# Forget gates' logits as four column tiles of 32 columns, in plain 32-bit, with a pattern that adds the partial sums

## The chip, the cores and the metric

One core of one Trainium2 chip runs the whole program. The metric is the device time of one execution in microseconds; smaller is better. TensorE multiplies matrices into eight banks of PSUM, VectorE (DVE) and ScalarE (ACT) work between PSUM and SBUF, GpSimd (POOL) computes and issues transfers, SyncE (SP) issues the transfers of weights.

## The reference

Two transformer blocks for 512 tokens of width 1024. The first modulates a normalised `x`, projects it and runs two attentions; the second has a convolution branch, a differential attention and a cross attention with a memory of 256 tokens. The change touches only the forget gates of the first block's first attention:

```python
h = rms_norm(x, g_pre[l]) * (1.0 + scale[:, None, :]) + shift[:, None, :]
proj = h @ w_in[l]
qa, ka, va, fa, za, qb, kb, vb, zb = jnp.split(proj, split_points, axis=-1)   # fa: 8 columns, one a head
...
cum = jnp.cumsum(jax.nn.log_sigmoid(f_logit.astype(jnp.float32)), axis=1)      # f_logit = fa + b_fgate
...
s = s + cb[..., None] - cum[:, :, None, :]
```

So the logits are `h` (512 x 1024) times eight columns of weights; their cumulated log-sigmoid is a bias on all scores of that attention.

## The kernel before

Almost all matrix products run in three matmuls of a rounded 32-bit type. Each operand is split into a high part (`hh`, `wh`) and a low part (`hl`, `wl`), and `three` adds lo x hi, hi x lo and hi x hi. The weights come in chunks of 1024 x 128 (0.52 MB), named by kind and number and listed in `CHUNKS` in the order in which they are multiplied. `("fa", 0)` holds the eight gate columns four times, at columns 0, 32, 64 and 96, with zeros between, so that the logits stand on four groups of partitions.

A chunk passes through three hands:

- SP loads it into one of four slots of `raw`, in the order of the list `RAW`, in which pieces of `w_ada` stand between chunks. SP's queue is one and strictly in order. A slot's next load waits until VectorE has split what was in it (`w_lo`), or, for a piece of `w_ada`, has added it up (`ada_used`). The names that share a slot here: `("va", 0)` follows the first chunk of the stage, `("va", 1)` the second; the order is chunk, chunk, `ada` 16, `ada` 17, `("va", 0)`, `("va", 1)`, `ada` 18, `ada` 19, `("va", 2)`, `("va", 3)`.
- ScalarE writes `wh` (its function `ahead`, L1126), then VectorE `wl` (its own `ahead`, L1800; the pieces of `w_ada` at L1781). Both go through their lists in order and stop only where the slot of `wh` and `wl` is not yet used up, so `ahead(name)` splits the chunk that stands four behind `name`.
- TensorE multiplies it: `chunk` takes eight times `three`, 24 matmuls of 512 columns. The four chunks `va` are multiplied in `wide`, where each step of 24 matmuls uses one chunk for all four tiles of tokens.

At the start of the first attention TensorE runs `fa`, `qa`, four steps of `va`, `ka`, then two plain 32-bit matmuls for the output gate (L652), then pieces of the chunks in `FILL` between the units of attention. The first scores wait for `cum_done`. In the meantime VectorE adds the bias to the logits (L1883), ScalarE takes absolute value, exponential and logarithm (L1282 to L1287), and VectorE the cumulated sum (L1889). ScalarE reads `qa` into `qf` and splits it (`raw_q`, L1294, and `split_q`, L1305).

GpSimd's queue in this stage: after `h_lo` it loads `sel` (its memory is that of `x` and `xT`, the scaled input in plain 32-bit) and twice `wmask`, then it stores `kvm`, 2 MB, to DRAM (L1046), then it computes angles.

`Banks` counts for each PSUM bank how often it was filled and emptied: `open` lets TensorE wait until the bank is empty, `wait_full` and `wait_empty` let others wait for it. `next_bank` hands out banks 0 and 1 in turn. Each engine executes its instructions in the order in which they stand.

Of the kernel before, what the change touches and what calls it, by code (L numbers as in the profile page):

```python
# [33 lines left out]
P = 128  # L34
# [18 lines left out]
K_COLS = K_DIST + S  # L53
# [14 lines left out]
CHUNKS += [("fa", 0), ("qa", 0)] + [("va", j) for j in range(4)] + [("ka", 0)]  # L68
# [71 lines left out]
for _h in range(4):  # L140
# [6 lines left out]
    "ones_in": "ones loaded", "sq_hi": "differential outputs' squares: hi", "sq_lo": "lo",  # L147
# [70 lines left out]
def constants():  # L218
    k = np.zeros((P, K_COLS), np.float32)
    b = np.zeros((P, 3 * P), np.float32)  # L220
    i = np.arange(P)
    k[:, K_IDENT:K_IDENT + P] = np.eye(P)
    k[:, K_BLOCKS:K_BLOCKS + P] = (i[:, None] // HD) == (i[None, :] // HD)
    k[:, K_ONES:K_ONES + P] = 1.0
    b[:, 0:P] = np.where(i[None, :] > i[:, None], 0.0, MASKED)
    b[:, P:2 * P] = np.where(i[None, :] <= i[:, None], 0.0, MASKED)
    b[:, 2 * P:3 * P] = np.eye(P)
    for n in range(8):
        for part in range(2):
            k[HD * (n % 2) + 32 * part + n, K_SEL + n // 2 * P:K_SEL + n // 2 * P + P] = 1.0  # L230
    back = i[:, None] + (S - P) - np.arange(S)[None, :]
    k[:, K_DIST:K_DIST + S] = np.where(back >= 0, -0.5 * back, MASKED)
    k[:, K_FREQ] = (10000.0 ** (-(i % (HD // 2)).astype(np.float64) / (HD // 2))).astype(np.float32)
    return k, b.astype(mybir.dt.np(BF16))
# [95 lines left out]
def build(nc, t, out):  # L330
    ctx = ExitStack()
    with ctx:
# [47 lines left out]
        dist, blocks, xk = shared([("dist", [P, S], F32), ("blocks", [P, P], F32)], [("xk", [P, 2, 2, MEM], F32R)])  # L380
# [84 lines left out]
        def _(pe):  # L465
# [179 lines left out]
            chunk(("fa", 0), H, split=s.h_lo)  # L645
            chunk(("qa", 0), H)
            wide("va", 0, H, [(tt, (2, 3, 4, 7)[tt]) for tt in range(T)])
# [352 lines left out]
        @block.sync  # L1000
        def _(sp):
            for tt in range(2):
                sp.dma_start(memx[:, tt, :], t["mem_2"][0, tt * P:tt * P + P, :]).then_inc(s.mem_in, 16)
            for name in RAW:
                last = RAW_BEFORE[name]
                if last is not None:
                    if last[0] == "ada":
                        sp.wait_ge(s.ada_used, last[1] + 1)
                    else:
                        sp.wait_ge(s.w_lo, NCH[last] + 1)  # L1010
                sp.dma_start(raw_rows(name), t["chunks"][STORED.index(("wo" if name[0] == "wp" else name[0], name[1]))])\
                  .then_inc(raw_loaded[RAW_SLOT[name]], 16)
            o_view = out[0].rearrange("(t p) d -> p t d", p=P)
            for half in range(2):
                for tt in range(T):
                    at = S * half
                    banks.wait_empty(sp, ("w2", half, tt))
                    sp.dma_start(o_view[:, tt, at:at + S], x1r[:, tt, at:at + S]).then_inc(s.out_sem, 16)
            sp.wait_ge(s.out_sem, 16 * 8)
# [3 lines left out]
        def _(pool):  # L1023
# [3 lines left out]
            for n, name in enumerate(("lambda_q1_2", "lambda_k1_2", "lambda_q2_2", "lambda_k2_2")):  # L1027
                pool.dma_start(lam4[:, n, :], t[name].partition_broadcast(P)).then_inc(s.bcast_in, 16)
            pool.dma_start(sinks[:], t["sinks"].partition_broadcast(P)).then_inc(s.bcast_in, 16)
# [8 lines left out]
            pool.wait_ge(s.h_lo, 8)  # L1038
            pool.dma_start(sel[:].rearrange("p a n -> p (a n)"), t["consts"][:, K_SEL:K_SEL + 4 * P].bitcast(F32R)).then_inc(s.sel_in, 16)
# [69 lines left out]
        def _(act):  # L1109
# [170 lines left out]
            act.wait_ge(s.cum_dve, 1)  # L1280
            f, e, l, cum = (cumt[:, n, :] for n in range(4))
            act.activation(e, f, ACT.Abs).then_inc(s.cum_act, 1)  # L1282
            act.wait_ge(s.cum_act, 1)
            act.activation(e, e, ACT.Exp, scale=-1.0).then_inc(s.cum_act, 1)
            act.wait_ge(s.cum_act, 2)
            act.wait_ge(s.ones_in, 16)
            act.activation(e, e, ACT.Ln, bias=ones[:, 0:1]).then_inc(s.cum_act, 1)  # L1287
            ahead(("fa", 0))

# [29 lines left out]
            split_q(0)  # L1319
            act.wait_ge(s.kvm_out, 16)  # L1320
            act.wait_ge(s.cum_dve, 2)
            act.activation(negcum[:], cum, ACT.Copy, scale=-1.0).then_inc(s.cum_hi, 1)
            for s_ in range(3):
                ahead(("va", s_))
# [431 lines left out]
        def _(dve):  # L1756
# [124 lines left out]
            key = ("fa", 0)  # L1881
            banks.wait_full(dve, key)
            banks.empty(dve.tensor_scalar(f, bank(key)[:], fbias, None, ALU.add), key)  # L1883
            banks.wait_empty(dve, key)
            dve.memset(l, 1.0).then_inc(s.cum_dve, 1)
            ahead(key)
            dve.wait_ge(s.cum_act, 3)
            then(dve.scalar_tensor_tensor(e, f, 0.0, e, ALU.min, ALU.subtract))
            dve.tensor_tensor_scan(cum, l, e, 0.0, ALU.mult, ALU.add).then_inc(s.cum_dve, 1)  # L1889
# [17 lines left out]
            split_q(0, 1)  # L1907
            dve.wait_ge(s.cum_hi, 1)
# [653 lines left out]
```

## Time and profile before

| | |
|---|---|
| median of 3 runs | 1158.21 us (1157.71 to 1159.0) |
| the profiled execution | 1158.44 us, span 1156.6 us |
| mean granted clock of TensorE | 0.996 |
| TensorE busy | 1123.9 us (97%), 5772 matmuls |
| VectorE busy | 823.7 us (71%) |
| ScalarE busy | 588.9 us (51%) |
| GpSimd busy | 66.1 us (6%) |

Times in the rows are microseconds from the start of the span, durations in microseconds or ns where the row says so. A row of the timeline has start, duration, engine, line, operation, tiles written and read, and how many were merged; brackets give idle time ahead of it and what ended it. The recorded duration of a matmul includes its way through the array, so the distance from one start to the next is what it costs. A plain 32-bit matmul leaves two records, one for each pass.

### The profile page before, as it was taken

Reading aid. Unit: us, or ns where it says so; the run is one execution under the profiler, and the core shown is the slowest. Engines: PE = TensorE matmul, PEld = TensorE weight load, DVE = VectorE, ACT = ScalarE, POOL = GpSimd, SP = SyncE. Lnnn points to the kernel's source line nnn. Section 1 sums busy time; section 2 is a strip of 40 time slices with the busy share of each in tenths; the row PEclk is TensorE's granted clock in tenths of the full one; section 3 lists DMA queues with packets and bytes.
Section 4 is the critical chain, followed back from the end, with each engine's and each line's share of the span. In section 5 each row is a group of like instructions: output and inputs, shape, how many; then the busy total and the mean of one; then the engine's idle time right before and its main releaser. Section 6 shows DMA issues by size and latency. Waiting matters only on the chain.

```text
span 1156.6 us, 15668 instructions
## 1 busy us (share of the span) xinstructions
PE 1123.9 (97%) x5772; PEld 917.3 (79%) x5772; DVE 823.7 (71%) x1423; ACT 588.9 (51%) x1084; POOL 66.1 (6%) x73
## 2 busy tenths in 40 slices
PE   5899999999999999999999999999999999999998
PEld 5898777776898877877778778888888888788887
DVE  5788555668566347999999985998888686853342
ACT  6663455456565455767766663424654223651230
POOL 2019500101000000000000000000000000000000
PEclk9899999999999999999999999999999999999999
DMA  9967321311355322212222133323222323223221
GB/s 340 364 211 260 128 70 65 92 64 38 130 170 195 107 73 73 73 37 91 75 91 87 56 128 113 103 80 110 73 73 96 124 89 107 91 78 111 89 76 73
DMA packets 35276, 130.20 MB, mean 113 GB/s; under 512 B 4272, under 2 KB 4656, under 8 KB 34688
## 3 DMA queue, kind: packets, MB, share of 16 engines
q1 hardware_dynamic: 31536, 112.74, 28.5%
q0 software_dynamic: 3376, 16.23, 4.2%
q8 instruction: 46, 0.75, 0.3%
q14 instruction: 30, 0.25, 0.1%
q10 hardware_dynamic: 288, 0.24, 0.1%
HBM read 121.59 MB, written 6.29 MB: 111 GB/s over the span
## 4 chain that ended last, share of the span: by engine, by line
PE 87%; DVE 5%; ACT 3%; issue 2%; DMA 2%; SPq 0%; POOL 0%; DVEq 0%; ACTq 0%
PE bank L474 26%; PE bank L476 26%; PE bank L475 26%; PE bank L576 2%; PE bank L725 2%; DMA raw<-in_chunks 2%; PE bank L846 1%; PE bank L753 1%; DVE wl L1800 1%; PE bank L679 1%; ACT qf L1207 1%; DVE ca L2211 1%; DVE stat L1955 0%; ACT wh L1126 0%; DVE cumt L2492 0%
## 5 line engine op out<-in xcount | busy, mean ns | idle before, releaser
L474 PE MATMUL bank<-hl,wh 128*128 128x512 f32 x888 | 358.9, 404 | 2.1 <-DVE u L2225 2.1
L476 PE MATMUL bank<-hh,wh 128*128 128x512 f32 x888 | 347.1, 391 | 0.0
L475 PE MATMUL bank<-hh,wl 128*128 128x512 f32 x888 | 346.3, 390 | 0.0
L1126 ACT ACTIVATE wh<-raw 128x1024 fp32r<-128x1024 f32 x185 | 191.9, 1057 | 204.6 <-PE bank L476 185.3
L1800 DVE TENSOR_TENSOR wl<-raw,wh 128x1024 fp32r<-128x1024 f32 x185 | 224.9, 1237 | 98.6 <-ACT wh L1126 97.9
L474 PEld LDWEIGHTS bank<-hl,wh 128*128 128x128 f32 x888 | 167.1, 188 | 39.2 <-issue 3.4
L476 PEld LDWEIGHTS bank<-hh,wh 128*128 128x128 f32 x888 | 166.7, 188 | 36.5
L475 PEld LDWEIGHTS bank<-hh,wl 128*128 128x128 f32 x888 | 167.1, 188 | 32.1 <-issue 1.4
L2211 DVE SCALAR_TENSOR_TENSOR ca<-u,vt,ca 128x512 f32<-128x512 f32 x232 | 157.9, 746 | 0.0
L475 PE MATMUL bank<-oh,wl 128*128 128x512 f32 (+1 forms) x256 | 93.9, 367 | 0.0
L476 PE MATMUL bank<-oh,wh 128*128 128x512 f32 (+1 forms) x256 | 93.9, 367 | 0.0
L474 PE MATMUL bank<-ol,wh 128*128 128x512 f32 x192 | 75.5, 393 | 0.0
L474 PE MATMUL bank<-wl,hh 128*128 128x512 f32 x160 | 63.2, 395 | 0.6 <-DVE hl L2129 0.6
L475 PE MATMUL bank<-wh,hl 128*128 128x512 f32 x160 | 62.3, 389 | 0.0
L476 PE MATMUL bank<-wh,hh 128*128 128x512 f32 x160 | 62.3, 389 | 0.0
L474 PE MATMUL bank<-wl,oh 128*128 128x256 f32 x192 | 55.7, 290 | 1.0 <-DVE ytok L2090 0.7
L475 PEld LDWEIGHTS bank<-oh,wl 128*128 128x128 f32 x256 | 49.4, 193 | 7.9 <-issue 0.5
L476 PEld LDWEIGHTS bank<-oh,wh 128*128 128x128 f32 x256 | 49.3, 193 | 7.5
L476 PE MATMUL bank<-wh,oh 128*128 128x256 f32 x192 | 55.0, 286 | 0.0
L2349 DVE SCALAR_TENSOR_TENSOR gj<-th,bank 128x512 f32<-128x512 f32 x16 | 11.0, 688 | 60.6 <-PE bank L476 56.3
L725 PE MATMUL bank<-cst,prob 128*128 128x128 f32 x248 | 42.5, 277 | 7.6 <-DVE prob L1977 5.2
L725 PEld LDWEIGHTS bank<-cst,prob 128*128 128x128 f32 x248 | 29.9, 140 | 23.7 <-DVE prob L1977 7.4
(329 smaller groups left out, 1660.3 us busy)
## 6 DMA issues: line engine op xcount, KB each, us to landing
raw<-in_chunks SPq DMA_DIRECT2D x193, 512.0 KB, 3.6
ada_a<-in_chunks SPq DMA_DIRECT2D x8, 512.0 KB, 11.5
ada_b<-in_chunks SPq DMA_DIRECT2D x8, 512.0 KB, 9.4
x<-in_x POOLq DMA_DIRECT2D x4, 512.0 KB, 10.3
mem_scratch<-kvm POOLq DMA_DIRECT2D x1, 2048.0 KB, 9.9
x<-in_x POOLq DMA_DIRECT2D x1, 2048.0 KB, 8.0
x_scratch<-x POOLq DMA_DIRECT2D x1, 2048.0 KB, 7.0
kvm<-mem_scratch POOLq DMA_DIRECT2D x1, 2048.0 KB, 9.9
```

The costliest lines, as they stand in the source:

```text
L474: pe.matmul(o, a[0], b[1], start=start, stop=False, **kw)
L475: pe.matmul(o, a[1], b[0], start=False, stop=False, **kw)
L476: return pe.matmul(o, a[0], b[0], start=False, stop=stop, **kw)
L576: ins = pe.matmul(ps[bank][:, 0:n], ones_[:], x_, start=i == 0, stop=i == len(squares) - 1)
L679: pe.matmul(ps[2 + side][:, at:at + w], qd[c % 2][half, q, q_], kp[c % 2][half, k, 0:w], start=(n, q, k) == (0, 0, 1), stop=n > 0, **({"sk ...
L725: ins = pe.transpose(ps[b][:, n * P:n * P + P], blk, ident[:])
L753: ins = pe.matmul(ps[7][half, cols], v_, p_, start=kb == 0, stop=True, skip_group_check=True)
L846: ins = pe.matmul(outs[u_, m], qd[j % 2][half, q, q_], kd[half, j % 2, k, 0:w], start=n == 0, stop=n == 2)
L1126: act.activation(wh[:, SLOT[nxt]], raw[:, RAW_SLOT[nxt]], ACT.Copy).then_inc(s.w_hi, 1)
L1207: act.activation(junk, src[:, tt, :], ACT.Square, accum_out=dst[:, tt:tt + 1]).then_inc(s.sumsq, 1)
L1800: dve.tensor_tensor(wl[:, w], raw[:, RAW_SLOT[nxt]], wh[:, w].bitcast(F32), ALU.subtract)\
L2211: ins = dve.scalar_tensor_tensor(dst, src, w, dst, ALU.mult, ALU.add)
```

## The change

- `CHUNKS` has `qa` ahead of `fa`. TensorE's order is now `qa`, gate logits, `va`, `ka`.
- `gate_logits` multiplies the raw 32-bit weights (`raw`, not `wh` and `wl`) with `xT`. Each of eight matmuls has 32 columns of weights: column tile `part` (output partitions 32 x `part` to 32 x `part` + 31) gets rows of features 2 x `part` and 2 x `part` + 1. The four tiles of the bank are then four partial sums of the same logits.
- ScalarE copies this bank to `cumt`, and after step 0 of `va` one matmul with the constant `fours` (1 where row and column are equal modulo 32) adds the four into bank 6, on all four groups of partitions. VectorE adds the bias from there.
- The absolute value, exponential, logarithm and cumulated sum come later in the orders of ScalarE and VectorE.
- SP waits for bank `("fa", 0)` before it loads into the slot of `fa`. GpSimd waits for it before `sel`, and loads `fours`.
- `("fa", 0)` is still split into `wh` and `wl`; nobody reads them.

```diff
-CHUNKS += [("fa", 0), ("qa", 0)] + [("va", j) for j in range(4)] + [("ka", 0)]
+CHUNKS += [("qa", 0), ("fa", 0)] + [("va", j) for j in range(4)] + [("ka", 0)]
...
+    k[:, K_FOURS:K_FOURS + P] = (i[:, None] % 32) == (i[None, :] % 32)
...
-            chunk(("fa", 0), H, split=s.h_lo)
-            chunk(("qa", 0), H)
-            wide("va", 0, H, [(tt, (2, 3, 4, 7)[tt]) for tt in range(T)])
+            def gate_logits():
+
+                wait_raw(pe, ("fa", 0))
+                b, w = next_bank(), RAW_SLOT[("fa", 0)]
+                banks.open(pe, b, ("fa", 0))
+                for i in range(2):
+                    for part in range(4):
+                        c, rows = 2 * part + i, slice(32 * part, 32 * part + 32)
+                        ins = pe.matmul(ps[b][rows, :], raw[:, w, c, rows], xT[:, c], start=i == 0, stop=i == 1,
+                                        skip_group_check=True)
+                banks.close(ins, ("fa", 0))
+                done_by[("fa", 0)] = ("fa", 0)
+
+            chunk(("qa", 0), H, split=s.h_lo)
+            gate_logits()
+            tiles = [(tt, (2, 3, 4, 7)[tt]) for tt in range(T)]
+            for s_ in range(4):
+                if s_ == 1:
+                    pe.wait_ge(s.fours_in, 16)
+                    banks.wait_empty(pe, ("fa", 0))
+                    banks.open(pe, 6, "logits")
+                    banks.close(pe.matmul(ps[6][:], fours[:], cumt[:, 1, :], start=True, stop=True), "logits")
+                used(wide_step("va", 0, s_, H, tiles), "va", 0, s_, tiles)
             chunk(("ka", 0), H)
...
+                if last == ("fa", 0):
+                    banks.wait_full(sp, last)
...
+            pool.dma_start(fours[:], t["consts"][:, K_FOURS:K_FOURS + P]).then_inc(s.fours_in, 16)
...
             pool.wait_ge(s.h_lo, 8)
+            banks.wait_full(pool, ("fa", 0))
...
             split_q(0)
+            f, e, l, cum = (cumt[:, n, :] for n in range(4))
+            banks.wait_full(act, ("fa", 0))
+            banks.empty(act.activation(e, ps[banks.where["fa", 0][0]][:], ACT.Copy), ("fa", 0))
+            ahead(("fa", 0))
             act.wait_ge(s.kvm_out, 16)
+            ahead(("va", 0))
+            act.wait_ge(s.cum_dve, 1)
+            act.activation(e, f, ACT.Abs).then_inc(s.cum_act, 1)
```

ScalarE's order behind the kernel's copy of the last `mv` bank, before. The first two rows split `("va", 0)` and `("va", 1)`; `bank0` is that of `qa`, and the third `wh` row, behind the logarithm steps, is `("va", 2)`.

```order
L1126 ACTIVATE wh<-raw 128x1024 [waits raw_loaded0,filled0]
L1126 ACTIVATE wh<-raw 128x1024 [waits raw_loaded1,filled0]
L1282 ACTIVATE cumt<-cumt 128x512 [waits cum_dve]
L1284 ACTIVATE cumt<-cumt 128x512 [waits cum_act]
L1287 ACT_TABLE_LOAD [waits ones_in]
L1287 ACTIVATE cumt<-cumt,ones_r 128x512 [waits cum_act]
L1126 ACTIVATE wh<-raw 128x1024 [waits raw_loaded0,filled1]
L1294 ACTIVATE qf<-bank0 128x512 [waits q_lo,filled0]
L1126 ACTIVATE wh<-raw 128x1024 [waits raw_loaded1,filled0]
L1305 ACTIVATE qk<-qf 128x512 [waits emptied0]
```

The same place after the change:

```order
L1152 ACTIVATE wh<-raw 128x1024 [waits raw_loaded0,filled0]
L1152 ACTIVATE wh<-raw 128x1024 [waits raw_loaded1,filled0]
L1310 ACTIVATE qf<-bank1 128x512 [waits q_lo,filled1]
L1152 ACTIVATE wh<-raw 128x1024 [waits raw_loaded0,filled1]
L1321 ACTIVATE qk<-qf 128x512 [waits emptied1]
L1338 ACTIVATE cumt<-bank0 128x512 [waits filled0]
L1152 ACTIVATE wh<-raw 128x1024 [waits raw_loaded1,filled0]
L1152 ACTIVATE wh<-raw 128x1024 [waits raw_loaded0,wide_used,kvm_out]
L1343 ACTIVATE cumt<-cumt 128x512 [waits cum_dve]
```

The new copy out of `bank0` (the partial sums) stands behind the splits of `("va", 1)` and `("va", 2)` and behind `split_q`; the logarithm steps moved from ahead of `("va", 2)` to behind the splits of `("va", 3)` and `("ka", 0)`.

SP's queue after the change, from the loads of the last `mv` chunks on. The row with `filled0` is `("va", 1)`; the next rows are `ada` 18 and 19, `("va", 2)` and `("va", 3)`, and so on.

```order
L1035 DMA raw<-in_chunks 128x1024 [waits w_lo] x7
L1035 DMA raw<-in_chunks 128x1024 [waits filled0,w_lo]
L1035 DMA raw<-in_chunks 128x1024 [waits ada_used] x2
L1035 DMA raw<-in_chunks 128x1024 [waits w_lo] x2
L1035 DMA raw<-in_chunks 128x1024 [waits ada_used] x2
```

Before, `("va", 1)` was one more of the loads that wait for `w_lo` alone.

## Rows read from the trace of the kernel before

**Rows 1.** The page's first part: span, then busy us, share, instructions.

```profile
span 1156.6 us, 15668 instructions
PE 1123.9 (97%) x5772; PEld 917.3 (79%) x5772; DVE 823.7 (71%) x1423; ACT 588.9 (51%) x1084; POOL 66.1 (6%) x73
```

**Rows 2.** Busy by stretch: PE, PEld, DVE, ACT, POOL (x), granted clock, DMA share, GB/s.

```profile
81.20:121.20 40.00, 40.00 (x175) 32.47 (x174) 33.09 (x32) 17.39 (x22) 33.12 (x20) 1.00 0.77 275
...
31.50:38.60 7.10, 5.46 (x26) 5.49 (x27) 6.80 (x8) 5.73 (x8) 0.00 (x0) 0.52 1.02 403
...
69.10:72.50 3.40, 3.40 (x18) 3.40 (x18) 3.33 (x9) 2.14 (x4) 0.00 (x0) 0.52 0.96 365
```

**Rows 3.** Timeline of TensorE, first matmuls of `qa`, of `va`, and around L652.

```profile
86.66 0.39 PE L474 MATMUL bank<-hl,wh 128*128 128x512 f32 x1
...
92.10 0.39 PE L474 MATMUL bank<-wl,hh 128*128 128x512 f32 x1
...
119.31 1.88 PE L652 MATMUL bank<-macc,ones_r 128*128 128x512 f32 x4
...
121.25 0.40 PE L475 MATMUL bank<-hh,wl 128*128 128x512 f32 x1
```

**Rows 4.** Timeline of TensorE, first value matmuls, on two column halves.

```profile
157.09 0.39 PE L476 MATMUL bank<-hh,wh 128*128 128x512 f32 x1
157.41 0.64 PE L753 MATMUL bank<-pair_a,va 128*64 128x512 f32 x1
157.42 0.64 PE L753 MATMUL bank<-pair_b,va 128*64 128x512 f32 x1
157.89 0.59 PE L753 MATMUL bank<-pair_a,va 128*64 128x512 f32 x1
...
158.32 0.49 PE L753 MATMUL bank<-pair_a,va 128*64 128x384 f32 x1
```

**Rows 5.** Timeline of ScalarE: split of `("va", 1)`, copy of `qa`, its split.

```profile
86.02 1.06 ACT L1126 ACTIVATE wh<-raw 128x1024 fp32r<-128x1024 f32 x1 [0.59 <-DMA raw<-in_chunks]
...
97.66 0.58 ACT L1294 ACTIVATE qf<-bank 128x512 f32<-128x512 f32 x1
...
99.09 0.62 ACT L1305 ACTIVATE qk<-qf 128x512 fp32r<-128x512 f32 x1
```

**Rows 6.** Tile `raw` on SP: loads issued at 87.2 and at 99.0.

```profile
L1011 SPq DMA_DIRECT2D raw<-in_chunks x1: 328/328/328, 87.2 to 87.2; - x1
...
DMA to landing us min/median/max: 9.4/9.4/9.4
...
L1011 SPq DMA_DIRECT2D raw<-in_chunks x1: 328/328/328, 99.0 to 99.0; - x1
...
DMA to landing us min/median/max: 3.4/3.4/3.4
```

**Rows 7.** Timeline of GpSimd's transfers.

```profile
78.52 0.54 POOL L1039 DMA_DIRECT2D sel<-in_consts  x1 [12.59 <-DVE hl L1865]
79.05 1.06 POOL L1041 DMA_DIRECT2D wmask<-in_consts_b  x2
86.54 0.54 POOL L1046 DMA_DIRECT2D mem_scratch<-kvm  x1 [6.43 <-DVE kvm L1872]
```

**Rows 8.** DMA queues (packets, MB, share): twice 87 to 94, 94 to 98.5, 79.5 to 84.5.

```profile
q0 software_dynamic: 130, 2.06, 82.8%
q1 hardware_dynamic: 124, 0.44, 15.7%
...
q1 hardware_dynamic: 485, 1.79, 99.3%
...
q1 hardware_dynamic: 240, 0.91, 56.0%
```

**Rows 9.** Timeline of VectorE: splits of `("va", 0)` and `("va", 1)`, then of `("va", 2)`.

```profile
85.97 2.83 DVE L1800 TENSOR_TENSOR wl<-raw,wh 128x1024 fp32r<-128x1024 f32 x2
...
97.79 1.23 DVE L1800 TENSOR_TENSOR wl<-raw,wh 128x1024 fp32r<-128x1024 f32 x1 [4.46 <-ACT wh L1126]
```

More of the change, by code:

```diff
@@ L52 @@
 K_DIST = 385 + 4 * P
-K_COLS = K_DIST + S
+K_FOURS = K_DIST + S
+K_COLS = K_FOURS + P
 VEC_ROWS = [("c", 8), ("b_ada", 16), ("g_pre", 8), ("norm_g", 8), ("mem_g", 8), ("dw_b", 8), ("ln_g", 8),
@@ L146 @@
 SIGNALS = {
-    "ones_in": "ones loaded", "sq_hi": "differential outputs' squares: hi", "sq_lo": "lo",
+    "ones_in": "ones loaded", "fours_in": "pattern that adds four partial sums loaded", "sq_hi": "differential outputs' squares: hi", "sq_lo": "lo",
     "const_in": "identity and frequencies loaded", "rows_in": "packed vectors loaded",
@@ L379, in build @@
         ident_b = sb("ident_b", [P, P], BF16)
-        dist, blocks, xk = shared([("dist", [P, S], F32), ("blocks", [P, P], F32)], [("xk", [P, 2, 2, MEM], F32R)])
+        dist, blocks, fours, xk = shared([("dist", [P, S], F32), ("blocks", [P, P], F32), ("fours", [P, P], F32)], [("xk", [P, 2, 2, MEM], F32R)])
         vt = sb("vt", [P, VT_COLS])
@@ L1278, in _ @@
                 ahead(("mv", 2 * g + 1))
[L1280 to L1288, printed above, removed]
             def raw_q(key, i, free, next_=True):
@@ L1319, in _ @@
             split_q(0)
+            f, e, l, cum = (cumt[:, n, :] for n in range(4))
+            banks.wait_full(act, ("fa", 0))
+            banks.empty(act.activation(e, ps[banks.where["fa", 0][0]][:], ACT.Copy), ("fa", 0))
+            ahead(("fa", 0))
             act.wait_ge(s.kvm_out, 16)
+            ahead(("va", 0))
+            act.wait_ge(s.cum_dve, 1)
+            act.activation(e, f, ACT.Abs).then_inc(s.cum_act, 1)
+            act.wait_ge(s.cum_act, 1)
+            act.activation(e, e, ACT.Exp, scale=-1.0).then_inc(s.cum_act, 1)
+            act.wait_ge(s.cum_act, 2)
+            act.wait_ge(s.ones_in, 16)
+            act.activation(e, e, ACT.Ln, bias=ones[:, 0:1]).then_inc(s.cum_act, 1)
+            ahead(("va", 1))
             act.wait_ge(s.cum_dve, 2)
             act.activation(negcum[:], cum, ACT.Copy, scale=-1.0).then_inc(s.cum_hi, 1)
-            for s_ in range(3):
-                ahead(("va", s_))
+            ahead(("va", 2))
             for tt in range(T):
@@ L1880, in _ @@
             f, e, l, cum = (cumt[:, n, :] for n in range(4))
[L1881 to L1889, printed above, removed]
             banks.wait_full(dve, ("qa", 0))
@@ L1907, in _ @@
             split_q(0, 1)
+            ahead(("fa", 0))
+            ahead(("va", 0))
+            banks.wait_full(dve, "logits")
+            banks.empty(dve.tensor_scalar(f, bank("logits")[:], fbias, None, ALU.add), "logits")
+            banks.wait_empty(dve, "logits")
+            dve.memset(l, 1.0).then_inc(s.cum_dve, 1)
+            dve.wait_ge(s.cum_act, 3)
+            then(dve.scalar_tensor_tensor(e, f, 0.0, e, ALU.min, ALU.subtract))
+            dve.tensor_tensor_scan(cum, l, e, 0.0, ALU.mult, ALU.add).then_inc(s.cum_dve, 1)
+            ahead(("va", 1))
             dve.wait_ge(s.cum_hi, 1)
```

## The prediction

> **What bounds the kernel now.** I read the page first, for shares: in one profiled execution of 1158.44 us (span 1156.6 us, so 1.8 us lie around it) TensorE is busy 97% of the span [rows 1]. Whatever lengthens or shortens TensorE's own sequence is therefore paid at full price, unless TensorE was idle there anyway. The next view is busy time by stretch, for the place of the change: from 81.2 to 121.2 us TensorE is busy 40.00 of 40.00 us at the full granted clock, VectorE 33.09, ScalarE 17.39, GpSimd 33.12 [rows 2]. So the stretch has no TensorE wait to recover, ScalarE has slack, and VectorE has little. Then the order of TensorE's work in time: a chunk's 24 matmuls take from 86.66 to 92.10, or 5.44 us, 0.227 us each; the plain 32-bit `ones` matmuls of the gate start at 119.31 and the work behind them runs from 121.25 [rows 3]. The gate-logit chunk `fa` is the one just ahead of it, from 81.2, and in both no wait stands.
>
> **What is removed and added on TensorE.** The 24 matmuls of `fa` go: -5.44 us. `qa` now starts at 81.2 in its place, with the same waits on `h_lo`, and ends at 86.66.
>
> The eight new matmuls are plain 32-bit, 128 rows by 32 columns by 512. No row has that shape. The nearest are the value matmuls, plain 32-bit with 64 columns [rows 4]: each leaves two records, a first pass at 157.41 and a second at 157.89, and the next matmul starts at 158.32, so two passes of 512 columns take 0.91 us. The other column half starts 0.01 us behind and costs nothing more. If four column tiles run side by side as two do, the eight are two rounds of 0.91, and with the 0.09 us before the first value matmul 1.9 us. If they don't overlap, eight times 0.91, 7.3 us. I take 1.9, since the nearest row shows overlap and the code puts the four tiles of a round next to each other. The Trainium skill bears on it ("TensorE: Matmul & The Clock Gate", Measured speedup vs the span model): three column tiles of 32 with 512 columns gave 2.38 times, not three times. Scaled to four tiles, an estimate from that page, the eight would take 7.3 / 3.2, 2.3 us and not 1.9; no run here shows it yet.
>
> The pattern matmul is one plain 32-bit matmul of 512 columns. Two such go in 119.31 to about 121.02 (121.25 less the one matmul of 0.23 that is between, whose record is long because it queues) [rows 3]: 0.86 each; I take 0.9 with the change of operands.
>
> So without a wait the change gives -5.44 + 1.9 + 0.9 = **-2.6 us**. The splits of `fa` into hi and lo on ScalarE and VectorE stay, since `fa` is still in `CHUNKS`; nothing is saved there.
>
> **What is moved, and past what.** The eight matmuls read `raw` itself, so three queues now wait for them.
>
> 1. SP may load `("va", 1)` into that slot only when bank `("fa", 0)` is full. Before, it waited for `w_lo` alone, and ScalarE had split it by 87.1 [rows 5]. Now the matmuls end at 86.66 + 1.9 = 88.6, with their drain 88.8. Behind it in the one SP queue stand two pieces of `w_ada` and `("va", 2)`, whose conditions have long been met; before, `("va", 2)` went out at 87.2 [rows 6]. Now the four go out at 88.8, 89.1, 89.5 and 89.8 (0.33 us an issue).
> 2. GpSimd's load of `sel` waits for the same bank, since `sel` shares the memory of `xT`. Before, it issued it at 78.52, the two `wmask` loads at 79.05, and the 2 MB store of `kvm` at 86.54 [rows 7]. Now `sel` 88.8, `wmask` 89.4, the store 90.5: the store falls right on the four loads instead of behind them.
> 3. ScalarE's own order: it splits `("va", 1)`, copies `qa`, then splits `("va", 2)`, then `split_q`, and only then copies the partial sums out of bank `fa`. TensorE's pattern matmul waits for that copy and stands ahead of `va` step 1, so all of TensorE's sequence waits. Before, the same splits stood in the same places, but no matmul waited for anything behind them.
>
> **When `("va", 2)` lands.** Alone, a 0.52 MB load takes 3.4 us (issued 99.0); the one issued at 87.2 beside the store took 9.4 [rows 6]. The reason is in the queues' rows [rows 8]: from 87 to 94 the store's queue moved 2.06 MB and the loads' queue 0.44 MB; from 94 to 98.5 the loads alone moved 1.79 MB, 0.40 MB/us; beside `sel` and `wmask`, from 79.5 to 84.5, they moved 0.91 MB, about 0.2 MB/us. Of the 3.4 us of a load alone 1.3 are bytes (0.52 / 0.40), and of the other 2.1 I put 1.3 ahead of the bytes: the new loads begin to move at 90.1. Until the store's packets start (by estimate 0.8 us after its issue, at 91.3) they move 0.25 MB. The store then takes some 6.5 us, until 97.8, in which they move another 0.25. The remaining 1.6 of 2.1 MB take 4.0 us: 101.8. The two guesses at starts can each be off by some tenths, so I take **101.5**. The bound from below is all four loads passing ahead of the store: 90.1 + (2.1 + 0.4) / 0.40 = 96.3. The Trainium skill ("DMA: Bandwidth & Descriptors", Queues, rings and completion order) says that an engine takes turns between queues by packets; with turns of equal bytes the loads would be through at about 100.5 here, 1 us sooner. The bytes of 87 to 94 are uneven, so the sum goes by them.
>
> **The stall.** After the landing ScalarE needs 1.06 for the split, 0.62 for `split_q` and 0.6 for the copy [rows 5]: 101.5 + 2.3 = 103.8. TensorE has then been through step 0 of `va` (its `("va", 0)` was there as before) since 88.6 + 5.44 = 94.0. The stall is **9.8 us** (4.6 at the lower bound). Nothing covers it.
>
> **The clock.** Early in the kernel TensorE waits more: from 31.5 to 38.6 it is busy 5.46 of 7.10 us, and the granted clock is 0.52 on average, the 1.2 GHz level: about 2.7 us lost. From 69.1 to 72.5, behind a stretch of one-column matmuls, it was 0.52 again: 3.4 x 0.48 = 1.6 us lost [rows 2]. A stall of 9.8 us brings the clock down inside the stall, and what follows starts at half: I take the middle, **+2.1 us**.
>
> **Does VectorE come last instead?** It splits in order, so it now idles from 87.2 (after `("va", 0)`) until ScalarE has split `("va", 1)`, near 95: before, it stood still 4.46 us at 97.79 instead, behind the cumulation, and was otherwise full [rows 9]. Of its 33.09 us in the stretch about 6 lie ahead of 87.2, so at most 27 are left, and not all of them are ahead of `cum_done`: 96 + 27 = 123, or 127 with some 4 us in which it waits for ScalarE's logarithm steps as before. TensorE wants `cum_done` for the first scores, which come behind the chunks at 121.25; 9 us later that is over 130. Hidden by 3 us or more in the main case. If the cover went (a stall of 4.6 and not 9.8), VectorE could come last by up to 2 us; the range holds that.
>
> **Sum:** -5.44 + 1.9 + 0.9 + 9.8 + 2.1 = **+9.3 us**. On 1158.44 this is 1167.7; the median of the three runs is 1158.2, 0.2 lower, so I say **1167.5**. About 0.2%, 2.3 us, is what a measurement of this kernel can tell from no change.
>
> **Rivals.**
> - *The loads pass the store.* For it: they go out first. Against: in [rows 8] the store's packets take four fifths of the bytes while they last. Landing 96.3, stall 4.6, clock 1.6: -2.6 + 4.6 + 1.6 = +3.6, 1161.8. Chance 0.20.
> - *The four column tiles don't overlap.* The eight take 7.3 instead of 1.9; everything behind moves by the same, and the stall stays: +5.4 on the main case, 1172.9. Against: [rows 4]. Chance 0.07.
> - *Not slower.* One mechanism: ScalarE gets to the copy while step 0 still runs, and the -2.6 us stays. Its price turns at a stall of 2.6 us, so `("va", 2)` would have to land by 94.3; it is issued at 89.8 and takes 3.4 alone, 93.2, so it needs both the store and the three loads ahead out of the way. With the landing at 93.2 the time is 1158.2 - 2.6 + 1.5 = 1157.1. Below 1155.9 (faster) the wait would have to be nothing. Chance 0.10, of which 0.06 within 0.2% and 0.04 faster.
> - *Main case*, the store first: 0.63.
>
> **Range.** The main case's own: landing 100 to 102.5, clock 1.6 to 2.7, the tiles 1.9 to 2.3, so 1165.3 to 1169.6. To leave no more than 2 in 10 outside I reach to the loads that pass: 1161 to 1170.5. Slower: 0.63 + 0.20 + 0.07 = 0.90.
>
> **What the profile after would show.** The eight matmuls near 86.7 in two rounds of four starts almost at once; the load of `("va", 1)` issued near 88.8 and four loads landing from 93 to 102 while the store's queue is busy; ScalarE idle for the DMA ahead of two splits, then the copy of the partial sums; TensorE idle once, from 94 to about 104, ahead of the pattern matmul, waiting for ScalarE; the clock at 0.5 for 3 to 5 us from there; everything from `va` step 1 on shifted by about 9 us and no more. A short idle at 94 with an early landing would be the first rival; eight starts 0.9 us apart the second; an idle ahead of the first scores instead would mean that VectorE came last, which I have not priced into the sum. I would be wrong most of all if `("va", 2)` lands early.

## The result: 1169.15 us, 11.2 us slower, and the profile after

The changed kernel takes 1169.15 us, the median of four runs (1168.21 to 1169.74). The kernel before takes 1157.96 us, the median of four (1156.94 to 1159.0). The ratio is 1.0094 with a 95% interval of 1.0081 to 1.0106. The prediction was 1167.5 in a range of 1161 to 1170.5.

The page of the kernel after, first part (busy us, share of the span, instructions), beside [rows 1]:

```profile
span 1166.4 us, 15660 instructions
PE 1123.3 (96%) x5766; PEld 914.0 (78%) x5766; DVE 823.8 (71%) x1423; ACT 589.2 (51%) x1085; POOL 66.4 (6%) x74
```

TensorE's busy sum is almost the same: the matmuls that went are paid back by others that ran at the lower clock. The span grew by 9.8 us: TensorE stood still for 10.4 us more (43.1 against 32.7) and was busy for 0.6 less. Busy time by stretch (us, PE, PEld, DVE, ACT, POOL, granted clock, DMA share, GB/s) shows where:

```profile
94.00:105.50 11.50, 0.16 (x1) 0.03 (x1) 4.14 (x4) 2.20 (x4) 10.91 (x8) 0.73 0.99 390
105.50:109.60 4.10, 4.10 (x8) 2.58 (x9) 4.10 (x4) 0.83 (x2) 3.93 (x3) 0.51 0.64 211
```

TensorE is still for 11.3 of 11.5 us, while the DMA engines are 0.99 busy. Then come 4.1 us at a granted clock of 0.51, the 1.2 GHz level. The timeline of TensorE of the kernel after names the wait:

```profile
86.53 1.92 PE L655 MATMUL bank<-xT,raw 128*32 128x512 f32 x16
88.38 0.50 PE L476 MATMUL bank<-wl,hh 128*128 128x512 f32 x1
...
93.77 0.39 PE L478 MATMUL bank<-wh,hh 128*128 128x512 f32 x1
105.50 2.05 PE L668 MATMUL bank<-cumt,fours 128*128 128x512 f32 x2 [11.34 <-ACT cumt L1338]
...
130.16 1.88 PE L674 MATMUL bank<-macc,ones_r 128*128 128x512 f32 x4
...
134.05 0.55 PE L701 MATMUL bank<-kp,qk 64*128 64x128 f32 x6
...
168.00 0.64 PE L775 MATMUL bank<-pair_a,va 128*64 128x512 f32 x1
```

The eight gate matmuls take 1.85 us, from 86.53 to the start of `va` step 0 at 88.38. The pattern matmul then waits 11.34 us for ScalarE's copy of the partial sums. The `ones` matmuls of the gate come at 130.16 instead of 119.31 [rows 3], and the first value matmul at 168.00 instead of 157.41 [rows 4], a shift of 10.6 us. Between them there is no large wait. The timeline of ScalarE tells why the copy is late:

```profile
91.97 1.06 ACT L1152 ACTIVATE wh<-raw 128x1024 fp32r<-128x1024 f32 x1 [8.13 <-DMA raw<-in_chunks]
...
103.30 1.06 ACT L1152 ACTIVATE wh<-raw 128x1024 fp32r<-128x1024 f32 x1 [9.78 <-DMA raw<-in_chunks]
...
104.78 0.58 ACT L1338 ACTIVATE cumt<-bank 128x512 f32<-128x512 f32 x1
```

The copy itself takes 0.58 us, and its operand was ready from 88.4 on. It stands in ScalarE's queue behind the splits of `("va", 1)` and `("va", 2)`, and both wait for loads. `("va", 1)` was split at 86.02 before [rows 5] and is split at 91.97 now. The transfers of tile `raw`, the last two of the four loads, and GpSimd's timeline:

```profile
L1035 SPq DMA_DIRECT2D raw<-in_chunks x2: 430/430/430, 89.4 to 89.9; - x2
...
DMA to landing us min/median/max: 8.7/11.0/13.3
```

```profile
89.21 0.54 POOL L1065 DMA_DIRECT2D sel<-in_consts  x1 [23.43 <-PE bank L655]
...
90.83 0.55 POOL L1072 DMA_DIRECT2D mem_scratch<-kvm  x1
```

`("va", 2)` is issued at 89.9 and lands 13.3 us later, at 103.2. The store goes out at 90.83, right behind it. The DMA queues (packets, MB, share) from 89 to 92, twice from 92 to 96, and twice from 96 to 103:

```profile
q1 hardware_dynamic: 214, 0.81, 80.5%
...
q1 hardware_dynamic: 193, 0.72, 55.0%
q0 software_dynamic: 172, 0.35, 39.7%
...
q0 software_dynamic: 179, 2.14, 72.1%
q1 hardware_dynamic: 223, 0.79, 29.0%
```

The loads have the engines to themselves first, then share them with `sel` and `wmask`, whose 172 small packets carry 0.35 MB. By 96 the loads' queue has moved 1.53 MB (the four loads are 2.1), and three of the four have landed by 98.1 (3.3, 4.2 and 8.7 us after their issue). From 96 on, the store takes 2.14 of 2.93 MB, and `("va", 2)`, the last of the four, crawls beside it.

### The profile page after: what moved, and what is told of

Its sections match the earlier page's. It is cut to its first block, busy times and chain, and to the rows that moved or that the text cites. A ratio compares the mean times of both kernels' runs of the same rounds, so it can differ in the third digit from the quotient of the medians.

```text
span 1166.4 us, 15660 instructions
## 1 busy us (share of the span) xinstructions
PE 1123.3 (96%) x5766; PEld 914.0 (78%) x5766; DVE 823.8 (71%) x1423; ACT 589.2 (51%) x1085; POOL 66.4 (6%) x74
## 4 chain that ended last, share of the span: by engine, by line
PE 85%; DVE 5%; ACT 4%; DMA 3%; issue 2%; SPq 0%; POOL 0%; DVEq 0%; ACTq 0%
PE bank L476 25%; PE bank L478 25%; PE bank L477 25%; DMA raw<-in_chunks 3%; PE bank L578 2%; PE bank L747 2%; PE bank L868 1%; PE bank L775 1%; DVE wl L1828 1%; PE bank L701 1%; ACT qf L1233 1%; DVE ca L2240 1%; DVE stat L1984 0%; ACT wh L1152 0%; SPq L1035 0%
## 5 line engine op out<-in xcount | busy, mean ns | idle before, releaser
L1828 DVE TENSOR_TENSOR wl<-raw,wh 128x1024 fp32r<-128x1024 f32 x185 | 224.0, 1232 | 103.2 <-ACT wh L1152 102.6
L1619 ACT ACTIVATE prob<-bank,stat 128x128 f32<-128x128 f32 (+3 forms) x64 | 32.9, 520 | 29.3 <-DVE stat L2277 29.3
```

What stands on the lines that cost most here:

```text
L1619: banks.empty(act.activation(prob[:, u_ % 2 if m == 0 else 2, 0:w], ps[banks.where[key][0]][:, 0:w], ACT.Exp, scale=-1.0, bias=stat[:, 0, ...
L1828: dve.tensor_tensor(wl[:, w], raw[:, RAW_SLOT[nxt]], wh[:, w].bitcast(F32), ALU.subtract)\
```

## Experiments

Every edit is to the kernel after unless it says otherwise. Medians stand beside the median of the kernel before on the same chip (1158.09 us for e1 to e4, 1158.06 for e5 to e8, 1157.87 for e9 and e10). Timelines give start, duration, instruction, and in brackets the idle time ahead and who ended it; `issue` there means that the profile names nobody.

### e1_copy_first: ScalarE copies the partial sums ahead of the late splits

```diff
@@ ScalarE, loop over mv @@
+                if g == 3:
+                    ahead(("mv", 7), NCH[("va", 1)])
+                    banks.wait_full(act, ("fa", 0))
+                    banks.empty(act.activation(cumt[:, 1, :], ps[banks.where["fa", 0][0]][:], ACT.Copy), ("fa", 0))
@@ behind split_q(0) @@
-            banks.wait_full(act, ("fa", 0))
-            banks.empty(act.activation(e, ps[banks.where["fa", 0][0]][:], ACT.Copy), ("fa", 0))
```

> The changed kernel, but ScalarE copies the partial sums right behind its split of (va, 1), ahead of the split of (va, 2). If the stall is a chain of two links (a late load of (va, 2), and the copy queued behind its split), only the second link goes: the pattern matmul starts near 94, and TensorE waits instead ahead of step 2 of va, from about 100.2 to 105.6 (landing 103.2, then 1.06 for ScalarE's split and 1.24 for VectorE's), 5.4 us where 11.3 were, with 1.5 to 2 us of half clock: near 1162.7. If ScalarE's order alone were the cause: the full -2.6 us, 1155.5. If VectorE's lateness comes last: an idle ahead of the first scores, and above 1163.

Measured: 1166.64 us, ratio 1.0076 (1.0061 to 1.0091). TensorE's timeline:

```profile
94.77 1.02 PE L668 MATMUL bank<-cumt,fours 128*128 128x512 f32 x2
...
107.31 0.80 PE L476 MATMUL bank<-wl,hh 128*128 128x512 f32 x1 [6.03 <-DVE wl L1830]
...
126.25 1.98 PE L674 MATMUL bank<-macc,ones_r 128*128 128x512 f32 x4 [0.77 <-DVE macc L1811]
...
133.09 0.55 PE L701 MATMUL bank<-kp,qk 64*128 64x128 f32 x6 [2.78 <-issue]
```

The wait ahead of the pattern matmul is gone, so the copy behind the late splits was its cause. But 2.5 of 11.2 us came back, not the 6 that I expected. TensorE meets the same late chunk one step on (6.03 us ahead of the matmuls with the split of `("va", 2)`), and 3.55 us more ahead of the output gate and the first scores. The first of these two is a wait for VectorE. For the second the profile names nobody; in e3 and e9 below, the same wait ends as VectorE's part of the keys is done. The clock also fell twice: 0.64 was granted from 107.3 to 112, and 0.76 from 133 to 140. In the changed kernel nothing of this showed, because the 11.3 us stall covered it.

The copy stands in this edit ahead of the split of `("va", 1)`, not right behind it as the expectation says: the trace has the copy at 89.29 and the split at 92.66. Here this costs nothing, since the chunk lands only then.

### e2_store_late: the 2 MB store goes out once `("va", 2)` is there

```diff
             banks.wait_empty(pool, ("mv", 3, 0))
+            pool.wait_ge(s.w_hi, NCH[("va", 2)] + 1)
             pool.dma_start(mem_scratch, kvm[:]).then_inc(s.kvm_out, 16)
...
-            act.wait_ge(s.kvm_out, 16)
             ahead(("va", 0))
...
             ahead(("va", 2))
+            act.wait_ge(s.kvm_out, 16)
```

> The changed kernel, but GpSimd stores kvm only when ScalarE has split (va, 2), and ScalarE waits for that store just ahead of its copies of va. If the store's packets delay (va, 2): the four loads (2.1 MB) and sel with wmask (0.4 MB) at about 0.4 MB/us land (va, 2) near 96, the stall falls from 11.6 to about 4.7, with 1.6 to 2 us of half clock: near 1162. If the four loads delay themselves and the store matters little: landing still after 101, near 1169.

Measured: 1164.68 us, ratio 1.0059 (1.0044 to 1.0074). ScalarE's and TensorE's timelines:

```profile
97.74 1.06 ACT L1153 ACTIVATE wh<-raw 128x1024 fp32r<-128x1024 f32 x1 [3.75 <-DMA raw<-in_chunks]
```

```profile
99.94 2.05 PE L668 MATMUL bank<-cumt,fours 128*128 128x512 f32 x2 [5.47 <-ACT cumt L1339]
...
130.13 0.55 PE L701 MATMUL bank<-kp,qk 64*128 64x128 f32 x6 [1.43 <-issue]
...
136.08 0.33 PE L747 MATMUL bank<-cst,prob 128*128 128x128 f32 x1 [1.62 <-DVE prob L1997]
```

With the store away `("va", 2)` is split at 97.74 instead of 103.30, so the collision with the store is worth 5.6 us of landing. The stall halves, to 5.47, and 4.5 us of the time come back, 2.7 fewer than expected. Small waits ahead of the output gate (0.23), the first scores and the next step, 3.3 us together, take part of the gain; there were 0.5 in the changed kernel.

### e8_copy_first_store_late: both edits together

> e1_copy_first and e2_store_late together. TensorE should have no idle ahead of the pattern matmul nor ahead of step 2 (landing near 97.5, split by 99.9, needed at 100.3). If VectorE, idle for 6 us or more behind the late (va, 1), sets a floor of its own, the time hardly falls below e2: 1163 to 1164.5, with the idle ahead of the output gate and the first scores grown to 5 us or more. If the stalls of TensorE were the cost by themselves: 1156 to 1157.

Measured: 1164.2 us, ratio 1.0057 (1.0042 to 1.0072). TensorE's timeline:

```profile
93.70 1.02 PE L668 MATMUL bank<-cumt,fours 128*128 128x512 f32 x2
...
124.06 3.78 PE L674 MATMUL bank<-macc,ones_r 128*128 128x512 f32 x4 [6.30 <-DVE macc L1812]
```

There is almost no stall among the chunks any more (0.95 us in one place), and the time hardly moves from that of e2, as expected. TensorE now waits 6.30 us for VectorE ahead of the output gate, and runs at a granted clock of 0.55 from 124 to 130. The timeline of VectorE shows what it stood still for:

```profile
92.69 1.23 DVE L1831 TENSOR_TENSOR wl<-raw,wh 128x1024 fp32r<-128x1024 f32 x1 [6.06 <-ACT wh L1153]
...
110.29 1.69 DVE L1831 TENSOR_TENSOR wl<-raw,wh 128x1024 fp32r<-128x1024 f32 x1 [5.29 <-ACT wh L1153]
```

This is a second floor under the first. VectorE idles for the late split of `("va", 1)` and for that of `("ka", 0)`, before it comes to the work that the output gate needs. So the time is 6 us above that of before even where TensorE's own stall is gone. Only part of this floor belongs to the change: the load of `("ka", 0)` is issued at 99.6 and takes 9.5 us, beside the store, which e2's edit sends out at 99.0.

### e7_before_sp_wait: the kernel before, with SP's new wait alone

```diff
+                if last == ("qa", 0):
+                    banks.wait_full(sp, ("fa", 0))
                 sp.dma_start(raw_rows(name), ...)
```

> The kernel before with one wait added: SP loads (va, 1) only when bank (fa, 0) is full (86.6, where the change has it at 88.6). Gate matmuls, orders of ScalarE and VectorE, and GpSimd's queue as before. If the late loads are what costs, this wait alone shows it: the load of (va, 1) goes out with the store beside it, lands near 96, VectorE idles from 87 to 97, and the kernel is 4 to 8 us slower, 1162 to 1166. If the late loads only hurt together with ScalarE's copy behind them, it stays within 1 us of 1158.

Measured: 1169.51 us, ratio 1.0101 (1.0086 to 1.0116). TensorE's waits from 76 us to the first value matmul (line, who was waited for: us in total, times, longest):

```profile
PE bank L474 <- DVE wl L1802: 6.2, 3, 5.3
PE bank L725 <- DVE prob L1969: 1.9, 1, 1.9
```

Nothing of the change's arithmetic is in this kernel: no new matmul, no copy that TensorE waits for. One wait in SP's queue, which holds four loads back until about the time of the store, costs 11.5 us, as much as the whole change does on balance. It does so by another path: TensorE waits for VectorE's splits of the late chunks, not for ScalarE's copy. I had expected 4 to 8. TensorE waits 8.1 us from 76 us to the first value matmul, against 0.8 before. Its busy time there, for the same work, is 83.79 us against 80.63 (by stretch, this kernel and the one before):

```profile
76.00:167.90 91.90, 83.79 (x411) 66.25 (x409) 58.40 (x80) 35.88 (x66) 39.53 (x28) 0.96 0.46 154
```

```profile
76.00:157.40 81.40, 80.63 (x418) 65.14 (x416) 58.88 (x82) 36.73 (x66) 44.15 (x28) 1.00 0.50 173
```

The 3.2 us more are the lower clock behind the stalls (0.96 on average against 1.00); with the 7.3 of waits they are the 10.5 us by which the first value matmul is later.

### e3_own_weights: the gate's weights in a place of their own

```diff
+        gw = mx[:, 0:C * 32].rearrange("p (c n) -> p c n", n=32)
-                        ins = pe.matmul(ps[b][rows, :], raw[:, w, c, rows], xT[:, c], ...)
+                        ins = pe.matmul(ps[b][rows, :], gw[:, c, :], xT[:, c], ...)
-                if last == ("fa", 0):
-                    banks.wait_full(sp, last)
+            pool.dma_start(gw, t["chunks"][STORED.index(("fa", 0))][:, 0:C * 32]...).then_inc(s.gw_in, 16)
```

The chunk `fa` is still loaded and split, as in the changed kernel; its stored rows now begin with the weights packed for `gw`.

> The changed kernel, but the gate weights are loaded once more by a small transfer into a place of their own (part of mx, not in use then), so that SP does not wait for the gate matmuls; the chunk fa is still loaded and split, GpSimd still waits ahead of sel. If SP's wait is the root: (va, 1) lands near 86 and (va, 2) near 92 (issued at 87.2, ahead of the store), the copy of the partial sums is done near 94.3, the stall is 0 to 1 us at full clock, and the time 1155.5 to 1156.5, faster than before. If the moved order of VectorE and ScalarE costs by itself (cum_done late): an idle ahead of the first scores and 1158 or more.

Measured: 1159.9 us (ten runs), ratio 1.0021 (1.0011 to 1.003). The timelines of ScalarE and TensorE:

```profile
89.71 1.06 ACT L1154 ACTIVATE wh<-raw 128x1024 fp32r<-128x1024 f32 x1 [3.16 <-DMA raw<-in_chunks]
```

```profile
93.32 1.02 PE L670 MATMUL bank<-cumt,fours 128*128 128x512 f32 x2
...
117.46 1.98 PE L676 MATMUL bank<-macc,ones_r 128*128 128x512 f32 x4 [1.31 <-DVE macc L1811]
...
124.29 0.55 PE L703 MATMUL bank<-kp,qk 64*128 64x128 f32 x6 [2.76 <-issue]
```

SP waits for nothing new, `("va", 2)` is split at 89.71, and the stall ahead of the pattern matmul is gone entirely. Most of the loss goes with it: 1159.9 against 1169.15. But the kernel is still 1.8 us slower than before and not 2.6 faster. The two idles shown are 4.07 us, where the kernel before had one of 0.77 in this stretch, and behind the second idle 5.21 us run at a granted clock of 0.67, which loses 1.7. That is -2.6 + 4.1 - 0.8 + 1.7 = +2.4; counted from the start of `qa` (80.29; that of `fa`, 81.19, before), the first value matmul is 2.6 us later. TensorE's gain is real here, and is more than taken back by these waits. The first is one for VectorE; the second ends at 124.29, right behind VectorE's `kp` (L1925, 123.51 and 0.68 long), which the scores read. `sel`, `wmask` and the store still wait for the gate matmuls in this kernel and go out from 88.37 to 89.98.

### e6 and e9: is it the store, or the copy's place?

e6 is e3 with GpSimd's store moved ahead of `sel` and `wmask`, so that it goes out at 85.39, as early as before (86.54). e9 is e6 with the copy early, as in e1.

> e3_own_weights, and GpSimd stores kvm ahead of sel and wmask, at the time it had before the change (near 86). If e3's loss against TensorE's sum (-2.6 expected, +1.8 measured) comes from the loads that ran beside the later store (9.9 us for (ka, 0), 4.5 us for a piece of w_ada), VectorE is on time again, the idle of 1.3 and 2.8 us ahead of the output gate and the first scores goes, and the time is 1155.5 to 1156.5. If it comes from the place of the logarithm steps in VectorE's and ScalarE's order alone, they stay and the time stays near 1159.5.

> e6_own_store_first, and ScalarE copies the partial sums right behind its split of (va, 1). e6 showed the store back at its old place delays (va, 2) to 94.5 and with it the copy queued behind its split (TensorE idle 3.3 us), which e3 had not; so e3's and e6's losses have two sources. Now neither the loads behind the store nor the copy's place should be left. If that was all: 1155.5 to 1157. If the later place of the logarithm steps in VectorE's order costs too, an idle ahead of the output gate or the first scores of 1 to 3 us stays and the time is 1158 to 1160.

Measured: e6 is 1161.24 us (seven runs), ratio 1.003 (1.0018 to 1.0041); e9 is 1161.19 (seven runs), ratio 1.0029 (1.0018 to 1.004). Both are above what either branch of their expectations gave. TensorE's timeline of e6, then of e9:

```profile
96.75 1.10 PE L670 MATMUL bank<-cumt,fours 128*128 128x512 f32 x2 [3.30 <-ACT cumt L1339]
```

```profile
118.34 1.98 PE L676 MATMUL bank<-macc,ones_r 128*128 128x512 f32 x4 [1.01 <-DVE macc L1812]
...
124.53 0.55 PE L703 MATMUL bank<-kp,qk 64*128 64x128 f32 x6 [2.12 <-issue]
...
130.21 0.33 PE L749 MATMUL bank<-cst,prob 128*128 128x128 f32 x1 [1.35 <-DVE prob L1999]
```

With the store early, `("va", 2)` is split at 94.55 in e6 instead of 89.71 in e3, and the copy behind its split stalls TensorE for 3.30 us. e9 takes that stall away and the time does not move. It has a `("va", 2)` that lands as early as before and an early copy, and still idles 4.48 us ahead of the gate, the scores and the next step. The timelines of ScalarE and of VectorE in e9 show what VectorE waits for:

```profile
89.02 0.60 ACT L1308 ACTIVATE cumt<-bank 128x512 f32<-128x512 f32 x1 [4.71 <-PE bank L657]
89.51 1.05 ACT L1153 ACTIVATE wh<-raw 128x1024 fp32r<-128x1024 f32 x1
```

```profile
90.60 1.23 DVE L1831 TENSOR_TENSOR wl<-raw,wh 128x1024 fp32r<-128x1024 f32 x1 [3.17 <-ACT wh L1153]
...
97.30 1.58 DVE L1831 TENSOR_TENSOR wl<-raw,wh 128x1024 fp32r<-128x1024 f32 x1 [2.29 <-ACT wh L1153]
...
107.03 0.74 DVE L1933 TENSOR_SCALAR cumt<-bank,vt 128x512 f32<-128x512 f32 x1
...
111.82 0.69 DVE L1937 SCALAR_TENSOR_TENSOR cumt<-cumt 128x512 f32<-128x512 f32 x1 [3.40 <-ACT cumt L1351]
...
123.75 0.68 DVE L1926 TENSOR_TENSOR kp<-bank,kp 128x512 fp32r<-128x512 f32 x1
```

Ahead of the work for the output gate VectorE idles 8.9 us here, where it idled 4.46 before ([rows 9], 97.79).

- 3.17 and 2.29 us, or 5.5, go to the splits of `("va", 1)` and `("va", 2)`. In e6 this is one wait of 5.80 us for `("va", 2)`. The early copy only cuts it in two: it stands ahead of the split of `("va", 1)`, not behind it as the expectation says, and makes ScalarE split at 89.51 what it splits at 84.52 in e6.
- 3.40 us go to ScalarE's logarithm steps, in e6 as well.

Before, VectorE had the same gap ahead of `("va", 2)`, but used it. It added the bias at 91.94 (0.74 us) and filled a tile with ones (0.48), then stood still for 4.46 us while ScalarE did the logarithm steps: 5.7 us together. Now the logits come out of the pattern matmul and the bias stands later in VectorE's order, at 107.03. The gap is as long and empty, and the 0.74, the 0.48 and the wait of 3.40 us come on top of it, 4.6 us. So VectorE is later with all that follows: TensorE's wait ahead of the first scores ends at 124.53, right behind `kp` (123.75 to 124.43), which stood at 120.21 before.

### e4_gates_first, e10_gates_first_five: own weights, and the gate computed ahead of `qa`

```diff
-CHUNKS += [("qa", 0), ("fa", 0)] + [("va", j) for j in range(4)] + [("ka", 0)]
+CHUNKS += [("qa", 0)] + [("va", j) for j in range(4)] + [("ka", 0)]
...
-            chunk(("qa", 0), H, split=s.h_lo)
+            pe.wait_ge(s.h_tmp, C)
             gate_logits()
+            chunk(("qa", 0), H, split=s.h_lo)
+            pe.wait_ge(s.fours_in, 16)
+            banks.wait_empty(pe, ("fa", 0))
+            banks.open(pe, 6, "logits")
+            banks.close(pe.matmul(ps[6][:], fours[:], cumt[:, 1, :], start=True, stop=True), "logits")
```

The pattern matmul moves here from `va` step 1, and no chunk `fa` is loaded or split. ScalarE copies the sums ahead of its splits of `va`, and the logarithm steps stand where they stood before the change. Both kernels are the same; e10 was timed again.

> As e3_own_weights, and the gate matmuls stand ahead of qa, fa is no chunk any more (neither loaded nor split), the pattern matmul stands ahead of va, and the logarithm steps stand where they stood before the change. TensorE's own sum says -2.6 us and no stall: 1155.5 or a little less. If the smaller work on ScalarE, VectorE and the queues gives something besides: 1154.5. If not faster than e3_own_weights by more than 0.5 us, the order of the logarithm steps cost nothing.

> The kernel of e4_gates_first with more rounds, since its interval (0.9985 to 1.0003) does not tell it from before, while its profile shows TensorE 2.6 us ahead at the output gate. If the 2.6 us reach the end: ratio 0.998, interval below 1. If part is lost behind the stage: ratio 0.999 with an interval that reaches 1.

Measured: 1156.79 us (ten runs), ratio 0.9994 (0.9985 to 1.0003), and 1156.51 us (eleven runs), ratio 0.9993 (0.9984 to 1.0002). TensorE's timeline of e4:

```profile
80.55 1.92 PE L657 MATMUL bank<-xT,mx 128*32 128x512 f32 x16
...
87.98 1.02 PE L667 MATMUL bank<-cumt,fours 128*128 128x512 f32 x2
...
89.08 0.40 PE L479 MATMUL bank<-wh,hl 128*128 128x512 f32 x1
...
116.10 1.88 PE L675 MATMUL bank<-macc,ones_r 128*128 128x512 f32 x4
```

From the first gate matmul to the output gate it takes 116.10 - 80.55 = 35.55 us. Before it was 119.31 - 81.19 = 38.12 (81.19 is the start of `fa` in the trace). The difference is -2.57, which is TensorE's sum without a wait (-5.44 + 1.9 + 0.9 = -2.64). At the end 1.3 and 1.4 us of it can be seen in the medians, 0.7 and 0.8 by the ratios, and both intervals reach past 1, so this version is not told apart from the kernel before. It is 3.1 us below e3, so by the expectation the order of the logarithm steps did cost something, though e4 also drops the chunk `fa`.

### e5_tile_by_tile: the eight matmuls in the other order

e3 with the two loops of the eight matmuls exchanged, so that both matmuls of a column tile follow one another.

> e3_own_weights with the two loops of the gate matmuls exchanged: both matmuls of a column tile next to each other, then the next tile. If a matmul overlaps the next only when that stands in another column tile, the starts go in a staircase and the eight take about 5 passes-of-two (each 0.86 to 0.91 us), 4.4 us and not 1.92. If TensorE reorders them freely they take 1.92 again. One look; the time is not asked for.

Measured: 1161.97 us in a single run. TensorE's timeline:

```profile
87.27 1.94 PE L657 MATMUL bank<-xT,mx 128*32 128x512 f32 x16
```

1.94 us against 1.92, where a staircase would have taken 4.4. TensorE overlaps the tiles in either order, and the order in the code buys nothing.

## Why the prediction was right, and where it wasn't

**TensorE's sum (-5.44 + 1.9 + 0.9).** Right in each term. The eight take 1.85 to 1.92 us, two rounds of two passes. The estimate that I had weighed from the Trainium skill ("TensorE: Matmul & The Clock Gate", Measured speedup vs the span model), its 2.38 times for three tiles scaled to four, gave 2.3 us and is 0.4 too high here: against the 7.3 that I worked out for eight in a row, 1.92 is 3.8 times. The pattern matmul takes 0.87 at full clock: in e4 it starts at 87.98 and the second matmul behind it at 89.08, and one of 0.23 lies between. e4 shows the whole sum, -2.57.

**SP's wait, and the order of the transfers.** Right. e7 shows that this wait alone can cost as much, +11.5, and e3 that most of the loss goes when it is taken away. Loads predicted from 88.8 to 89.8 went out from 88.6 to 89.9, the store at 90.83 (90.5).

**The landing of `("va", 2)`, 101.5.** It was 103.2, so the size was near, but the order behind it was another, and this part of the hit is luck. I had the loads move 0.25 MB until 91.3, at the rate that they have beside `sel` and `wmask`; then the store, which I took to have the engines until 97.8; then 1.6 MB of loads alone. In the run the loads had 1.53 MB through by 96, and three of the four had landed by 98.1. The store stands behind `sel` and `wmask` in GpSimd's queue. Their 172 packets held the engines 40% of the time from 92 to 96, and the store's bytes moved mostly from 96 on, beside the last load. The two orders end near each other because the sum of bytes is nearly the same in both: 2.1 MB of loads, 2.1 of store and 0.4 of `sel` and `wmask` at 0.40 MB/us are 11.5 us from 90.1, or 101.6. The rival in which the loads pass the store is thus true for three of the four and false for `("va", 2)`, the one that counts; e2 confirms that the store holds it up, since with the store away its split comes 5.6 us sooner.

Landing by turns of equal bytes, the estimate that I took from the Trainium skill ("DMA: Bandwidth & Descriptors", Queues, rings and completion order), would have been 100.5, further off: from 96 to 103 the store's queue took 2.14 MB and the loads' 0.79. The Trainium skill itself speaks there of turns by packets, and with that the traces agree. From 97 to 102 the store's queue moved 109 packets and the loads' 107, and in the kernel before, from 91 to 93, they moved 34 and 35. The bytes were 1.79 against 0.41 MB and 0.56 against 0.14, because a packet of the store carries 16 KB there and one of the loads 4.

**The stall, 9.8.** 11.3 by the bracket, 11.6 from the end of step 0 at 93.9 to 105.5. The difference is the later landing: 103.2 for 101.5.

**The clock, +2.1.** 4.10 us at a granted clock of 0.51 lose 4.10 x 0.49 = 2.0.

**Together** -5.44 + 1.9 + 0.9 + 11.6 + 2.0 is +11.0. The first value matmul is 10.6 us later, the span of the profiled execution 9.8 us longer, and the median 11.2 us higher. The path was right: the late loads, ScalarE's copy behind their splits, and TensorE's one stall. The miss of 1.65 us is the stall's size. (The ends of the inner range, 1165.3 and 1169.6, are 0.2 and 0.1 off their own terms, which changes nothing.)

**VectorE "hidden by 3 us or more", and late "by up to 2 us" if the cover went.** In the changed kernel it was hidden, as said: the bracket ahead of the first scores is empty. The second half was wrong. With TensorE's stall at the pattern matmul taken away (e1), the time stayed 8.5 us above before, and with the late chunk out of the way too (e8) still 6.1, with 6.30 us of waiting for VectorE ahead of the output gate, in part brought on by the moved store. I had counted VectorE's busy time up to `cum_done` and looked for its lateness at the first scores alone; in e8 it shows sooner, at the output gate, whose `macc` comes behind the same splits in VectorE's order. The 4.46 us at 97.79 [rows 9] I put "behind the cumulation"; they stand ahead of the scan at 100.06, where VectorE waits for ScalarE.

**"Not slower", if `("va", 2)` lands by 94.3.** This turning point was wrong. In e3 the chunk is split at 89.7 and no stall is left, and the kernel is still 1.8 us slower; e9 is 3.3 slower. What I had left out of it is VectorE: a lower floor lies below the stall. The logarithm steps, which now depend on the pattern matmul, no longer fill VectorE's gap ahead of `("va", 2)` and cost it some 4.6 us later (e9), and TensorE then waits for VectorE ahead of the output gate and the scores. In e3 late loads come on top: VectorE waits 4.51 us for one piece of `w_ada` that lands beside the store. The first rival's 1161.8 was too low as well. e2 comes near it, with a stall of 5.47, and took 1164.68; there too the waits behind the stall were missing from my sum.

**What stays open.** The logarithm steps were not moved by themselves; their 4.6 us are read off the traces of e6, e9 and before. Of the 3.3 us that e9 loses, its trace shows 1.7 up to the first value matmul, counted from the start of the stage. e4 is level with the kernel before, but it changes several things at once: the gate matmuls first, the logarithm steps in their old place, and no chunk `fa` to load and split. Which of them it needs is not shown. Nor is it shown why 2.57 us on TensorE in e4 and e10 are only 1.3 and 1.4 in their medians. Counted from the start of the stage, their first value matmul is still 2.3 and 2.4 us sooner than before. From there to the end the profiled executions take 999.2 us (before), 998.4 (after), 1000.1 (e4) and 1000.9 (e10), so the unchanged rest alone differs by 2.5 us from one execution to another.

## What to carry to other kernels

A new consumer that reads a load slot directly makes the slot's next load wait for it, and with it everything behind that load in the same queue. Price the queue, not the matmul: here 2.6 us were to be won on TensorE, and one wait on SP cost 11.5. When a stall is large, look at what it covers before you count its removal as a gain: each floor here (11.2, then 8.5 with the copy early, then 6.1 with the store late too) came into sight only once the one above was gone. And look at what the experiment itself brings in: e8's late store delayed another chunk. The saving came through on TensorE, as far as the output gate, only in the kernel in which the small weights had memory of their own and the new result was computed early enough that its long chain on two other engines kept its old start.

## What the runs showed of the hardware that was not expected

- The order of the eight column-tile matmuls does not matter: 1.92 us round by round, 1.94 tile by tile. The second matmul of a column tile does not hold back the first of the next tile in the queue.
- The small transfers are not small in time: `sel` and `wmask` moved 0.35 MB and took 39.7% of the engines' time from 92 to 96 us, or 1.6 of 4 us; the store took 72.1% of 7 us, or 5.0, for 2.14 MB. Per byte they cost about twice as much (4.5 against 2.4 us a MB).
- Two queues with work on the same engines moved as many packets each (109 and 107 from 97 to 102 us), whatever a packet held. The store's queue, with packets of 16 KB, had 1.79 of 2.20 MB.
- A 0.52 MB load that takes 3.3 us to land by itself (the first of the four, issued at 88.6) takes 13.3 as the fourth, with the store issued a microsecond behind it.
